# A hybrid decoder layer: rotated parts held in PSUM, single-column finds, and one more split on GpSimd

## What is computed

```
proj = h @ w_in[l] + b_in[l]
dq, dk, dv, iq, ik, iw, sq, sk, sv = jnp.split(proj, offsets, axis=-1)
dq = apply_rope(dq...); dk, iq, ik, sq, sk the same
o_dsa = dsa_sparse_attention(dq, dk, dv, iq, ik, iw)
o_swa = swa_sink_attention(sq, sk, sv, swa_sinks[l])
mix = jnp.concatenate([o_dsa, o_swa], axis=-1) @ w_o[l]
h = layer_norm(DEEPNORM_ALPHA * h + mix, ln1_g[l], ln1_b[l])
c = memory_cross_attention(h, mem, ...)
h = layer_norm(DEEPNORM_ALPHA * h + c, ...)
m = squared_relu_mlp(h, w_up[l], w_down[l])
h = layer_norm(DEEPNORM_ALPHA * h + m, ...)
```

## Time and profile before

| | us |
|---|---|
| median of 3 runs | 1621.69 (1620.58 to 1622.23) |
| profiled execution | 1621.91 |
| its span, first to last instruction | 1620.1 |
| PE busy | 1517.6 (94%) |
| DVE busy | 891.6 (55%) |
| POOL busy | 554.2 (34%) |
| ACT busy | 475.3 (29%) |

### The profile page before, as it was taken

The page is one execution under the profiler, slowest core; times in us unless marked ns, Lnnn a source line. Parts: engine busy times, 40 slices in busy tenths (PEclk is TensorE's granted clock), DMA queues, the critical chain, the costliest instruction groups (busy, mean ns, idle before and its releaser), DMA issues.

```text
span 1620.1 us, 20754 instructions
## 1 busy us (share of the span) xinstructions
PE 1517.6 (94%) x7720; PEld 1290.6 (80%) x7720; DVE 891.6 (55%) x1751; ACT 475.3 (29%) x1007; POOL 554.2 (34%) x554
## 2 busy tenths in 40 slices
PE   7998888888979999989999999999999999999996
PEld 6877667878869988778887788888888888888884
DVE  7578879788894332693427733333333333333357
ACT  3025467788636641121301211111110101111010
POOL 5240257655620003343223253333333333333300
PEclk9999999999979999999999999999999999999998
DMA  6445145545410013221010221111111111011001
GB/s 226 156 150 150 65 169 170 183 144 157 150 46 27 1 71 112 98 75 36 28 53 1 88 71 51 52 53 52 52 53 52 53 52 48 31 53 53 0 26 78
DMA packets 61331, 128.96 MB, mean 80 GB/s; under 512 B 6960, under 2 KB 34096, under 8 KB 53552
## 3 DMA queue, kind: packets, MB, share of 16 engines
q1 hardware_dynamic: 44208, 100.37, 18.7%
q10 hardware_dynamic: 17024, 27.27, 4.7%
HBM read 100.35 MB, written 27.26 MB: 79 GB/s over the span
## 4 chain that ended last, share of the span: by engine, by line
PE 73%; DVE 15%; ACT 5%; issue 4%; DMA 2%; ACTq 1%; POOL 0%; SPq 0%; DVEq 0%; POOLq 0%
PE banks L705 21%; PE banks L707 21%; PE banks L706 21%; PE banks L904 3%; PE banks L759 2%; PE banks L891 2%; PE banks L760 2%; ACT unread_late L1107 2%; PE banks L913 1%; DVE h_buf L1866 1%; DVE unread L1544 1%; DVE bn L1852 1%; ACT band_prob L1203 1%; DVE score L1511 1%; ACT unread_early L1107 1%
## 5 line engine op out<-in xcount | busy, mean ns | idle before, releaser
L691 POOL TENSOR_SCALAR w_hi<-raw 128x512 fp32r<-128x512 f32 x268 | 174.3, 678 | 884.0 <-PE banks L707 660.4
L696 POOL TENSOR_TENSOR w_lo<-raw,w_hi 128x512 fp32r<-128x512 f32 x268 | 364.3, 1393 | 0.0
L1966 DVE TENSOR_TENSOR h_buf<-h_buf,banks 128x1024 f32<-128x1024 f32 x112 | 136.7, 1221 | 145.8 <-PE banks L707 145.8
L705 PE MATMUL banks<-act_hi,w_hi 128*128 128x512 f32 x512 | 199.3, 389 | 1.7 <-DVE act_lo L1845 1.7
L705 PE MATMUL banks<-w_hi,hid_hi 128*128 128x512 f32 x512 | 199.3, 389 | 1.4 <-DVE hid_lo L1946 1.4
L706 PE MATMUL banks<-act_lo,w_hi 128*128 128x512 f32 x512 | 199.2, 389 | 0.0
L706 PE MATMUL banks<-w_lo,hid_hi 128*128 128x512 f32 x512 | 199.2, 389 | 0.0
L707 PE MATMUL banks<-act_hi,w_lo 128*128 128x512 f32 x512 | 199.2, 389 | 0.0
L707 PE MATMUL banks<-w_hi,hid_lo 128*128 128x512 f32 x512 | 199.2, 389 | 0.0
L1335 ACT ACTIVATE relu_buf<-banks 128x512 f32<-128x512 f32 x64 | 38.3, 599 | 521.6 <-PE banks L707 521.6
L1941 DVE TENSOR_TENSOR relu_buf<-relu_buf 128x512 f32<-128x512 f32 x64 | 45.2, 707 | 239.8 <-ACT relu_buf L1335 239.8
(11 more groups left out here) (181 smaller groups left out, 2824.7 us busy)
## 6 DMA issues: line engine op xcount, KB each, us to landing
raw<-w_up_dram SPq DMA_DIRECT2D x16, 1024.0 KB, 4.8
raw<-w_down_dram SPq DMA_DIRECT2D x16, 1024.0 KB, 4.8
q_tile<-qk_dram SPq DMA_DIRECT2D x176, 64.0 KB, 2.2
qk_dram<-q_hi ACTq DMA_DIRECT2D x28, 256.0 KB, 2.0
qk_dram<-roped ACTq DMA_DIRECT2D x28, 256.0 KB, 2.3
x_raw<-x_t_dram SPq DMA_DIRECT2D x8, 512.0 KB, 8.6
raw<-wk_mem_dram SPq DMA_DIRECT2D x4, 1024.0 KB, 5.4
raw<-wv_mem_dram SPq DMA_DIRECT2D x4, 1024.0 KB, 5.2
```

Of the source, the lines that this page charges most:

```text
L691: pool.tensor_scalar(w_hi[s][:, col], raw[c % 2][:, col], 1.0, 1.0, ALU.mult, ALU.mult)\
L696: pool.tensor_tensor(w_lo[s][:, col], raw[c % 2][:, col], w_hi[s][:, col].bitcast(F32), ALU.subtract).then_inc(w_ready, 1)
L705: pe.matmul(dst, lh, rh, start=(first and n == 0), stop=False)
L1966: dve.tensor_tensor(h_buf[:, t, :], h_buf[:, t, :], ring_l[n % 2][:], ALU.add)\
```

## The change

It has three parts. `POOL_SPLIT` goes from 7 to 6, so the low part of unit 6 is made by POOL, before chunk 6 of the weights, and ACT stores it one unit later. For units 9 to 12 the product of the second half goes to `swa_out`, a bank of PSUM, in place of `rot_part`. And in the bisection `find_refused` is called once for each column, all finds ahead of the first `set_next`, each of which waits for its own find.

```diff
-POOL_SPLIT = 7
+POOL_SPLIT = 6
+ROT_IN_PSUM = range(max(INDEX_HALVES) // 2 + 1, len(ROPE) - 1)
...
-            split_before = {C_DQ: (7,), C_DQ + 1: (8, 9), C_MEM: (10, 11), C_MEM + 1: (12,), C_MEM + 2: (13,)}
+            split_before = {C_DQ: (6, 7), C_DQ + 1: (8, 9), C_MEM: (10, 11), C_MEM + 1: (12,), C_MEM + 2: (13,)}
...
+                turned = swa_out if r in ROT_IN_PSUM else rot_part[:]
...
-                c1 = then(dve.scalar_tensor_tensor(out=rot_part[:], in0=src, scalar=b, in1=sin[:, tok],
+                c1 = then(dve.scalar_tensor_tensor(out=turned, in0=src, scalar=b, in1=sin[:, tok],
...
-                dve.tensor_tensor(roped[s][0][:], roped[s][0][:], rot_part[:], ALU.subtract)\
+                dve.tensor_tensor(roped[s][0][:], roped[s][0][:], turned, ALU.subtract)\
...
-                dve.scalar_tensor_tensor(out=rot_part[:], in0=src, scalar=b, in1=cos[:, tok],
+                dve.scalar_tensor_tensor(out=turned, in0=src, scalar=b, in1=cos[:, tok],
...
-                dve.tensor_tensor(roped[s][1][:], roped[s][1][:], rot_part[:], ALU.add).then_inc(rope_done, 1)
+                dve.tensor_tensor(roped[s][1][:], roped[s][1][:], turned, ALU.add).then_inc(rope_done, 1)
...
-                        dve.wait_ge(dve_step, then(dve.tensor_scalar(refused[:, 0:n], count[:, 0:n], 0.0, float(1 << k),
-                                                                     ALU.is_lt, ALU.mult)))
+                        found_at = [then(find_refused(c, k, 0.0)) for c in range(n)]
                         for c in range(n):
+                            dve.wait_ge(dve_step, found_at[c])
                             set_at[c] = then(set_next(c, k))
```

## The result

The changed kernel takes 1611.8 us (median of four runs, 1610.8 to 1613.9) against 1622.0 us (four runs, 1620.6 to 1624.6) for the kernel before in the same comparison: a ratio of 0.9937 [0.992, 0.9954]. The profiled execution took 1611.8 us, with a span of 1609.9 against 1620.1.

What follows compares the result with a forecast made beforehand. While the last units are rotated no engine is full; a chain of waits through several engines sets the pace, and it changes between ACT, PE and DVE in attention. 1621.9 - 5.2 (ring) - 2.7 (attention) = 1614.0 us; range 1609.5 to 1619.0.

Steps and rivals of the forecast that it cites:

- The ring: Repeating chain through DVE and ACT while the last units are rotated; the change saves 5.2 us there.
- 4 x 0.06: Finds in the ring: more instructions cost 0.06 us per step in four turns, 0.2 us lost.
- rival D: Ring and attention: one-column finds are held by POOL as well, so the kernel is slower, 1630 us; chance 0.04.
- Part 3: Unit 6 split by POOL, about 126 to 130 us: PE does not wait there, so costed at nothing.
- The attention stage: Banded attention and memory products, up to some 430 us: column finds save 2.7 us, with ends of 0 and 7.
- All that the turns save therefore arrives at this point: PE's first memory product, at 259.41 us after 4.67 us idle: the ring's saving arrives there, 5.2 us.
- Its term for part 1: Turned part of units 9 to 12 in PSUM: L1473 falls from 1.75 to 0.69 us, four times, 4.2 us.
- 1.0 + 2.7: Finds column by column: 1.2 us gained less 0.2 lost in the ring, and 2.7 us in the attention stage.
- A: The attention stage gives nothing but its end, 1.0 us: 1615.7 us, or 1617 with none; chance 0.15.
- B: In the attention stage DVE's relief moves ACT's counts up too, 7 us: 1609.7 us; chance 0.10.
- C: In the ring L1473 stays at 1.75 us, or writes to PSUM eat the gain: 1618.2 us; chance 0.09.
- breaks even near 1624: Finds beside POOL's subtractions: with half of rival D's loss on the path, the change breaks even near 1624 us.

Runs made afterwards that it cites:

- Part 1 alone: Kernel before, with only the turned part of units 9 to 12 put in PSUM: 1619.45 us, ratio 0.9992 [0.9983, 1.0000].
- the early finds: Two-column finds of the ring done column by column; added to the PSUM edit of units 9 to 12, three-column finds whole: 0.9979 of the kernel before.
- the last one: Kernel before, with the turned part of units 8 to 13 in PSUM and column finds only in the attention stage: 0.9943 [0.9931, 0.9955].
- Part 2 alone: Kernel before, with only the finds of the bisection done column by column: 1615.91 us, ratio 0.9968 [0.9955, 0.9980].
- one table: Kernel before 1; turned part of units 9 to 12 in PSUM 0.9992; attention-stage finds by column 0.9981; both 0.9939.
- the other: Kernel before 1; turned part of units 9 to 12 in PSUM 0.9992; all finds by column 0.9968; both 0.9951, again 0.9951.
- the two-column kernel: Changed kernel, each find working on two neighbouring columns instead of one: 1.0017 [1.0006, 1.0027] of the kernel before.
- Part 1 with whole late finds: Turned part of units 9 to 12 in PSUM, attention-stage finds left whole; against the kernel before 0.9992, or 0.9979 with ring finds by column.
- part 1 and late finds: Kernel before, with the turned part of units 9 to 12 in PSUM and column finds only in the attention stage: 0.9939 [0.9924, 0.9954].

## Why the prediction was right, and where it wasn't

**The ring.** Its steps hold: L1473 of units 9 to 12 at 0.69 us with those of SBUF still at 1.75; a period of 13.61 us (forecast 13.6); writes to PSUM 0.75 and 0.76 us, as the SBUF ones in the earlier trace rows, so the value taken was right; finds at 0.14 us. Part 1 alone shortens the ring by 4.87 us and the early finds by 1.31, together 6.2 where 5.2 were forecast. Two terms make the difference. The memory subtraction took 2.29 us in place of 3.04 at its new place in time, which the prediction had not priced. And a step with more finds is no longer than one with few: the first bit starts 0.17 us after them (222.91 to 223.08), as free ones did in the earlier trace rows, so 4 x 0.06 was not lost. (Further finds do cost: with each column's find issued three times, 0.045 us for each one added.) The rule of one SBUF operand, which the Trainium skill states (SBUF — State Buffer, Who interferes with whom), is borne out: the additions with an operand in PSUM took 687 ns at the median, four in the changed kernel and six in the last one. Its sentence on two-port mode says that `tensor_scalar` can enter it, and rival D priced single-column finds by that. At one column no find is held (166, none over 147 ns); at two columns some are, as the sentence allows.

**Part 3** gives nothing, as forecast, and PE's stretch before 140 us is as it was.

**The attention stage is the step that failed**, though the sum of 1614.0 us came out 2.2 us from the measurement. "All that the turns save therefore arrives at this point" is right for the memory product; that it also arrives at the end was assumed, not said. The prediction wrote 1621.9 - 5.2 - 2.7 with each term standing by itself. Its term for part 1 was 4.2 us. Alone, part 1 arrives at the memory product with 5.05 us and leaves the attention stage with 0.7; over all runs it gives 1.3 us, so the term was too large by 3. The early finds lose likewise: with part 1 they shorten the ring by 6.2 us, and the kernel is 3.4 us faster. Part 2 alone gives 5.2 us where 1.0 + 2.7 were forecast, 1.5 more, which is within the interval. And a surplus of the pair, 5.5 us in one table and 1.5 in the other, stands nowhere in the sum. That the total came out is in part luck: too much for the one and too little for the rest cancelled.

The mechanism that was missed: finds meet POOL's runs of subtractions on DVE, and an edit that shifts the stage deals anew which one meets a run, and how early in it. One find shows it, the one of 3.70 us, with 2.35 us of lead lost in its stretch. It doesn't explain the 1.98 us lost ahead of it. Nor is the stage free of it once the finds are: the 5.64 us of L1773 in the changed kernel are the same thing at another instruction. So why more of the shift arrives with finds by column is argued from this one find and not shown.

**Rivals.** A (only the end gives) and B (7 us from relief) both priced one stage whatever came before it, so neither is what happened. B's cause, that ACT's counts move up when DVE is free, fits the one held find, behind which ACT stood idle for 5.17 us; nothing here shows it for the rest. C is refuted by 687 ns. D's mechanism is real, for two columns. Against the kernel before it was priced at 1.5 us less up to the memory product and 10 more in attention; the two-column kernel's profile has 4.9 less and 12.0 more, and the median is 3.2 us above (1625.1 against 1622.0). The prediction's "breaks even near 1624" was a slip: 1624 is 2 us slower than the kernel before.

**What stays open.** Part 1 with whole late finds has attention stages of 343.19 and 342.20 us, against 338.80 and 339.94 without part 1; the one held find is about half of the first. In the second, the early finds, the largest hold is 2.61 us and the lead runs out over several tiles, from 7.9 us at the first to 3.3 at the sixth. The granted clock may have a part in it: summed over stretches of 5 us from 240 to 600 us, as twice the share missing from 1, time at 1.2 GHz was 61.3 us before, 57.8 with part 1, 63.4 with early finds, 47.7 with part 1 and late finds, 44.4 and 57.8 in the changed kernel's two profiles. Over the 13 profiles other than the two-column kernel's this goes with the stage's length (correlation 0.80, 0.4 us of stage for each). Whether it is a cause or a result wasn't separated.

## What to carry to other kernels

Where DVE and POOL meet, make the DVE instruction one that isn't held: in these runs one with an operand in PSUM, or a single column in place of three, even if that makes three instructions of one. Small is not enough: 8 columns with two SBUF operands were held for 5.64 us. When a stage is shifted by some microseconds, a saving ahead of it is not yet a saving at the end: follow it at a few fixed events (outputs of tiles) through the stage. And test two edits alone and together before their gains are added, with enough runs to tell the surplus from the noise; here one table of four told it and the other did not.

## What the hardware showed unexpectedly

- **One column is different in kind from two.** 128x1 finds: 135 to 147 ns in 166 of 166 beside the same work of POOL; 128x2: 153 to 3686 ns in 83.
- **A held instruction need not get in at the next boundary.** The three-column find at 313.39 us waited through the boundaries of POOL's subtractions, 3.70 us, to the end of the run. L1773 in the changed kernel waited for all four of a run, 5.64 us. Others got in at the next one: the find at 375.49 us in the kernel before took 1.18 us and ended inside POOL's run of four (374.10 us, 5.02 us long).
- **PSUM as destination costs DVE nothing here:** 0.75 and 0.76 us for 128x512 fp32 against 0.75 in SBUF.
